# Modulation vectors computed beside later matmul phases instead of in an opening of their own

## The reference, cut to what matters

```python
cond = jax.nn.silu(c)
for l in range(DEPTH):                                   # DEPTH = 2
    ada = (cond @ ada_w[l] + ada_b[l])[:, None, :]       # ada_w[l] is 1024 x 6144, 25 MB
    sh1, sc1, g1, sh2, sc2, g2 = jnp.split(ada, 6, axis=-1)
    h = rms_norm(x, norm1_g[l]) * (1.0 + sc1) + sh1
    x = x + g1 * mixer_sublayer(h, positions, ...)       # 4 token mixers, gates, w_o
    h = rms_norm(x, norm2_g[l]) * (1.0 + sc2) + sh2
    f = swiglu(h, ...) if l % 2 == 0 else moe_swiglu(h, ...)
    x = x + g2 * f
```

## Time and profile before

| | |
|---|---|
| three runs | 6308.77, 6313.16 (median), 6316.53 us |
| profiled execution, span (its own time; the profile gives no other) | 6307.7 us |
| PE busy | 5470.3 us, 87% of the span |
| DVE, ACT, POOL busy | 37%, 30%, 28% |

### The profile page before, as it was taken

The page is one execution under the profiler, slowest core; times in us unless marked ns, Lnnn a source line. Parts: engine busy times, 40 slices in busy tenths (PEclk is TensorE's granted clock), DMA queues, the critical chain, the costliest instruction groups (busy, mean ns, idle before and its releaser), DMA issues. The chain is left out here.

```text
span 6307.7 us, 75191 instructions
## 1 busy us (share of the span) xinstructions
PE 5470.3 (87%) x29832; PEld 4556.7 (72%) x29833; DVE 2332.4 (37%) x1993; ACT 1908.7 (30%) x1541; POOL 1757.5 (28%) x506
## 2 busy tenths in 40 slices
PE   3778779987999977877998499999989999889995
PEld 2527557766778753765776398998989898788984
DVE  8344321113102124432111254433464446654455
ACT  0112111113212111211111144343354345543453
POOL 0130111113344313011111142252354145432442
PEclk6779999998999987999999599999999999999997
DMA  9201011122333320101112256555586557865577
GB/s 388 75 0 27 14 38 46 46 84 78 90 112 96 111 86 0 27 14 37 46 46 85 92 182 205 193 187 187 180 272 207 186 186 261 291 220 192 174 249 251
DMA packets 731573, 829.44 MB, mean 131 GB/s; under 512 B 17362, under 2 KB 646226, under 8 KB 731090
## 3 DMA queue, kind: packets, MB, share of 16 engines
q1 hardware_dynamic: 722306, 792.39, 38.7%
q10 hardware_dynamic: 4560, 18.88, 0.8%
q0 software_dynamic: 4608, 16.78, 0.7%
HBM read 782.89 MB, written 45.09 MB: 131 GB/s over the span
## 5 line engine op out<-in xcount | busy, mean ns | idle before, releaser
L1806 POOL TENSOR_TENSOR e_w_lo<-e_raw,e_w_hi 128x2048 fp32r<-128x2048 f32 x170 | 993.7, 5845 | 1650.3 <-ACT e_w_hi L1742 1650.3
L247 POOL TENSOR_TENSOR w_lo<-w_raw,w_hi 128x1024 fp32r<-128x1024 f32 (+1 forms) x260 | 612.7, 2358 | 2480.2 <-ACT w_hi L242 2480.2
L253 PE MATMUL banks<-h_hi,w_hi 128*128 128x512 f32 x2688 | 1086.9, 404 | 191.1 <-POOL w_lo L247 126.4
L254 PE MATMUL banks<-h_lo,w_hi 128*128 128x512 f32 x2688 | 1057.5, 393 | 0.0
L255 PE MATMUL banks<-h_hi,w_lo 128*128 128x512 f32 x2688 | 1056.5, 393 | 0.0
L253 PE MATMUL banks<-e_x_hi,e_w_hi 128*128 128x256 f32 x3584 | 1020.2, 285 | 35.0 <-issue 26.2
L254 PE MATMUL banks<-e_x_lo,e_w_hi 128*128 128x256 f32 x3584 | 1019.2, 284 | 0.0
L255 PE MATMUL banks<-e_x_hi,e_w_lo 128*128 128x256 f32 x3584 | 1019.1, 284 | 0.0
L1742 ACT ACTIVATE e_w_hi<-e_raw 128x2048 fp32r<-128x2048 f32 x340 | 648.4, 1911 | 511.0 <-PE banks L255 413.5
L253 PEld LDWEIGHTS banks<-h_hi,w_hi 128*128 128x128 f32 x2688 | 511.4, 190 | 326.5 <-issue 154.2
L253 PEld LDWEIGHTS banks<-e_x_hi,e_w_hi 128*128 128x128 f32 x3584 | 693.4, 193 | 38.3 <-issue 28.7
(11 more groups left out here) (276 smaller groups left out, 6303.7 us busy)
## 6 DMA issues: line engine op xcount, KB each, us to landing
e_raw<-in_moe_w_dram SPq DMA_DIRECT2D x508, 1024.0 KB, 5.1
w_raw<-in_ffn_w_dram SPq DMA_DIRECT2D x120, 512.0 KB, 3.8
w_raw<-in_w_in_dram SPq DMA_DIRECT2D x108, 512.0 KB, 4.0
ada_w<-in_ada_w_dram SPq DMA_DIRECT2D x16, 3072.0 KB, 13.2
e_io<-row_scratch SPq DMA_DIRECT2D x13, 1024.0 KB, 6.7
y_scratch<-e_io ACTq DMA_DIRECT2D x12, 1024.0 KB, 4.2
x_res<-x_scratch SPq DMA_DIRECT2D x16, 512.0 KB, 5.5
w_br<-in_w_branch_dram SPq DMA_DIRECT2D x64, 128.0 KB, 3.8
```

The costliest lines, as they stand in the source:

```text
L247: pool.tensor_tensor(m.w_lo[b][:, 0:kt, :], m.w_raw[b][:, 0:kt, :], m.w_hi[b][:, 0:kt, :].bitcast(F32), ALU.subtract).then_inc(s.lo_ready, 1)
L253: pe.matmul(out, wh, rh, start=first, stop=False)
L254: pe.matmul(out, wh, rl, start=False, stop=False)
L1806: eng.tensor_tensor(by_k(w_lo[u]), half_block(q, h), by_k(w_hi[u]).bitcast(F32), ALU.subtract).then_inc(lo_sem[q], 1)
```

## The change

- The opening makes only the first 16 columns of 128 of layer 0's modulation (shift and scale of the first norm): four blocks of 512 columns. `x` is turned half by half straight into `m.x`, where it stays; ACT squares it from PSUM, PE sums the squares, ACT takes the root and DVE the reciprocal there.
- Layer 0's `norm_project_phase` neither loads `x` nor sums squares. SP stores `x` to `xs` after the first two weight blocks, then loads the positions; the rope angles are made by DVE after blocks 1 to 3 and 5 to 7, the sines by ACT after its rounding of blocks 4 and 8. Its loops are written out for both layers.
- The other 32 columns of 128 of layer 0 are made in layer 0's `gate_phase`, one of 128 columns in each of the 32 blocks: SP loads 512 KB, DVE multiplies (128x1024) and reduces over the 8 row tiles. PE sums them over partitions at the start of `out_proj_phase`.
- Layer 1's modulation is made in layer 0's `ffn_phases`: 256 columns (1 MB) in each of the 22 steps of the first half, and two more after the steps of the second half. DVE multiplies and reduces 128x2048; PE sums.

```diff
@@ opening_phase
+            for n, (half, k) in enumerate(steps):
+                if k == 0:
+                    pe.wait_ge(x_in[half], 16)
+                if n >= 4:
+                    pe.wait_ge(s.copied, n - 3)
+                    pe.wait_ge(s.squared, n - 3)
+                for t in range(4):
+                    last = pe.transpose(...)
+                last.then_inc(s.turned, 1)
+                if n:
+                    total(n - 1)             # waits squared; one 512-column product with ones
+            total(len(steps) - 1)
+            for j in range(NB):              # NB = 4
+                pe.wait_ge(s.added, j + 1)
...
+                if j == NB - 2:              # DVE, after block 2
+                    dve.wait_ge(s.root, 1)
+                    dve.reciprocal(rstd[:, :, :], rstd[:, :, :]).then_inc(s.inv, 1)
@@ norm_project_phase, SP of layer 0
+            for j in range(2):
+                w_load(sp, s, m, j, j, w_view(w, cols[j]))
+                for k in range(KT):
+                    sp.dma_start(a.xs[P * k:P * (k + 1), :], m.x[:, k, :]).then_inc(s.stored, 16)
+                sp.wait_ge(s.stored, 16 * KT)
+                sp.wait_ge(s.lo, KT)
+                sp.dma_start(pos_i[:, :], ...).then_inc(s.p_in, 16)
+            for j in range(2, nblocks):
+                w_load(sp, s, m, j, j % 2, w_view(w, cols[j]))
@@ gate_phase, layer 0: SP, then DVE, after each block's own work
+                        sp.wait_ge(s.ada_mult, NBR * mt + n + 1)
+                        sp.dma_start(ada_raw[n % 2][:, :, :], ...)
+                        dve.tensor_tensor(ada_prod[:, :, :], ada_raw[b][:, :, :], cond_wide(m, P), ALU.mult).then_inc(s.ada_mult, 1)
+                        dve.tensor_reduce(m.ada_part[...], ada_prod[:, :, :].rearrange("p k n -> p n k"), AX.X, ALU.add)
@@ out_proj_phase, layer 0: PE, ahead of its blocks
+                for i in range(48 - ADA0):
+                    last = pe.matmul(m.ps[:, 7, i:i + 1], m.ada_part[:, P * i:P * i + P], ones_column)
@@ ffn_phases, layer 0, first part
 SP:
+                def ada_load(j):
+                    sp.wait_ge(s.ada_sum, j + 1)
+                    sp.dma_start(ada_raw[:, :, :], w_view(a.ada_w[l + 1], AW * j, AW)).then_inc(s.ada, 16)
                 with sp.Fori(0, FT) as f:
                     ...                      # the two w_load of step f
+                    if half == 0:
+                        ada_load(f)
 PE:
+                def ada_total(j, at):
+                    pe.wait_ge(s.ada_sum, j + 2)
+                    for i in range(2):
+                        last = pe.matmul(m.ps[:, 7, ds(2 * at + i, 1)], ada_sum[:, P * i:P * i + P], ones_column)
                         ...                  # the 48 matmuls of step f
+                        if half == 0:
+                            ada_total(2 * i + c, 2 * i + c)
 DVE:
+                def ada_part(j):
+                    dve.wait_ge(s.ada, 16 * j + 16)
+                    dve.tensor_tensor(ada_raw[:, :, :], ada_raw[:, :, :], cond_wide(m, AW), ALU.mult).then_inc(s.ada_mult, 1)
+                    dve.wait_ge(s.ada_mult, j + 1)
+                    dve.wait_ge(s.ada_out, j + 1)
+                    dve.tensor_reduce(ada_sum[:, :], ada_raw[:, :, :].rearrange("p k n -> p n k"), AX.X, ALU.add).then_inc(s.ada_sum, 1)
+                dve.sem_inc(s.ada_sum, 1)
                         ...                  # hid, hid_hi, hid_lo of step f
+                        if half == 0:
+                            ada_part(f)
+                if half == 1:
+                    for j in (0, 1):
+                        ada_part(j)          # then bias and scale of layer 1
```

More of the change, by code:

```diff
@@ L113, in constants @@
     return c
+ADA0 = 16
 SEM0 = 104
@@ L282, in opening_phase @@
     cst = m.const
-    GRP = 6
-    W = P * GRP
-    NB = 6 * D // W
+    W = HALF
+    NB = ADA0 * P // W
     xrow = m.place("x_rows", [P, ST, D], F32, m.R)
[L287 to L297, removed]
+    sq = [m.place(f"o_sq{b}", [P, HALF], F32, m.R + (32 + 2 * b) * KB) for b in range(2)]
+    part_sum = [m.place(f"ada_part{b}", [P, W], F32, m.R + (36 + 2 * b) * KB) for b in range(2)]
@@ L299, in _ @@
+    wb = [m.place(f"ada_w{j}", [P, KT, W], F32, m.R + o * KB) for j, o in enumerate((136, 152, 88, 40))]
+    rstd = m.rstd0
+    with phase(nc, "c_in", "id_in", "x_in0", "x_in1", "w0", "w1", "w2", "w3", "turned", "copied", "squared", "totals", "root", "inv",
+               "silu", "scaled", "added", "summed", "folded") as (block, s):
+        w_in = (s.w0, s.w1, s.w2, s.w3)
+        x_in = (s.x_in0, s.x_in1)
+        steps = [(half, k) for half in range(NHALF) for k in range(KT)]
         @block.sync
@@ L303, in _ @@
[L303 to L308, removed]
+            for j in range(NB):
+                sp.dma_start(wb[j][:, :, :], w_view(a.ada_w[0], j * W, W)).then_inc(w_in[j], 16)
@@ L310, in _, with total @@
         @block.tensor
         def _(pe):
[L312 to L319, removed]
+            def total(n):
+                half, k = steps[n]
+                pe.wait_ge(s.squared, n + 1)
+                pe.matmul(m.ps[:, 6 + half, :], cst[:, K_ONE:K_ONE + P], sq[n % 2][:, :],
+                          start=(k == 0), stop=(k == KT - 1)).then_inc(s.totals, 1)
@@ L325, in _ @@
                                      cst[:, K_ONE:K_ONE + 1], start=True, stop=True)
                 last.then_inc(s.summed, 1)
+        @block.scalar
+        def _(act):
+            act.wait_ge(s.c_in, 16)
+            act.activation(m.small[:, S_COND:S_COND + KT], m.small[:, S_COND:S_COND + KT], ACT.Silu).then_inc(s.silu, 1)
+            for n, (half, k) in enumerate(steps):
+                act.wait_ge(s.turned, n + 1)
+                act.activation(m.x[:, k, half * HALF:(half + 1) * HALF], m.ps[:, n % 4, :], ACT.Copy).then_inc(s.copied, 1)
+                if n >= 2:
+                    act.wait_ge(s.totals, n - 1)
+                act.activation(sq[n % 2][:, :], m.ps[:, n % 4, :], ACT.Square).then_inc(s.squared, 1)
+            act.wait_ge(s.totals, len(steps))
+            act.activation(rstd[:, :, :], m.ps[:, 6:8, :], ACT.Sqrt, bias=cst[:, K_EPS:K_EPS + 1], scale=1.0 / D).then_inc(s.root, 1)
@@ L387, in _ @@
[L387 to L407, removed]
@@ L1199, in gate_phase @@
     w = a.w_in[l]
-    with phase(nc, "raw0", "raw1", "br0", "br1", "hi_ready", "lo_ready", "mm_done", "sig_ready", "gated", "summed") as (block, s):
+    ada = l == 0
+    if ada:
+        ada_raw = [m.place(f"g_ada_raw{b}", [P, KT, P], F32, m.R + (136 + 4 * b) * KB) for b in range(2)]
+        ada_prod = m.place("g_ada_prod", [P, KT, P], F32, m.Z0 + 42 * KB)
+    with phase(nc, "raw0", "raw1", "br0", "br1", "hi_ready", "lo_ready", "mm_done", "sig_ready", "gated", "summed",
+               "ada0", "ada1", "ada_mult", "ada_sum") as (block, s):
         @block.sync
@@ L1306, in _ @@
             credit_pe(pe, s)
+            if l == 0:
+                for i in range(48 - ADA0):
+                    last = pe.matmul(m.ps[:, 7, i:i + 1], m.ada_part[:, P * i:P * i + P], m.const[:, K_ONE:K_ONE + 1], start=True, stop=True)
+                last.then_inc(s.ada_sums, 1)
             for j in range(KT):
```

268 lines of the change are left out of this document (173 added, 95 removed).

## The result

Predicted 6481 us (6430 to 6560). The changed kernel takes 6498.18 us (median of four, 6495.6 to 6506.16) against 6313.59 (four, 6308.77 to 6316.53) of the kernel before: 1.0297 times, 95% interval 1.0284 to 1.031. Its profiled span is 6504.4, that of before 6307.7; the profiled execution is the slowest of the four.

What follows compares the result with a forecast made beforehand. PE was taken to bound the FFN steps, DVE the opening's end. Terms -110.3 - 23.4 + 2.6 + 2.4 + 229 + 5.8 + 46 + 16.1 = +168: span 6476, median 6481 us (6430 to 6560).

Steps and rivals of the forecast that it cites:

- The order of the FFN steps: FFN first half: PE waits for DVE's reduction of the same step, a serial chain of 10.9 us, 21 times: +229.
- The sum: Whole kernel: all terms together +168, span 6307.7 to 6476; median 5.5 above the span, so 6481 us.
- rival 3: Opening: PE stays at half clock, so it gains 94 in place of 110.3; whole 6498 us; chance 6%.
- The reduction: FFN steps: DVE's 128x2048 reduction taken as one plain pass, 2.30 us, with no such row to read.
- rival 1: FFN steps: the reduction, reading with a 1 KB step, is slow; at twice the time, 4.6, whole 6537; chance 10%.
- The clock: FFN first half: PE restarts at half clock after each 10 us gap, 2.2 per step, 21 times: +46 (29 to 61).
- The opening: Start of the kernel: with fewer modulation columns made, it ends at 67.4 in place of 177.74 us: -110.3.
- T: Opening: the time at which the 16 steps of transposing and squaring x end, put at 44.5 us.
- its steps go at ACT's 1.3: Opening: variant in which PE's steps keep ACT's pace of 1.3 us in place of 1.5: -113.
- Layer 0's norm: Layer 0 before its first matmul: loading x, squares, root and reciprocal go; 10.5 us left of 33.9: -23.4.
- Gate phase and output projection: Layer 0: only the last gate block's pair is exposed, +2.6; 64 sum records before the output projection, +2.4.
- Second half's tail: FFN second half: the two last pieces stand behind `hid_lo`, the second loading only after the first is reduced: +16.1.

Runs made afterwards that it cites:

- e1: Changed kernel, with DVE making the piece of modulation ahead of its step's hidden block in the FFN steps: 6219.48 us, 0.9853 of the kernel before.
- e5: Changed kernel, FFN reduction summing 8 neighbouring elements in place of 8 lying 1 KB apart (sums wrong, only timing read): 6482.15 us, one run.
- e6: Changed kernel, FFN reduction replaced by three additions of contiguous halves: 6476.92 us, 1.0255 of the kernel before.
- e9: Changed kernel, plus 50 matmuls of 512 columns into an unused bank in each first-half FFN step, before PE's wait: 6466.53 us, 1.0249.
- e2: Changed kernel, plus 40 matmuls of 512 columns into an unused bank in each first-half FFN step, before PE's wait: 6565.17 us, 1.0402.
- e8: As e1, with twelve pieces in each FFN half; in the opening PE sums blocks 0 and 1 between steps, reciprocal after block 3: 6187.71 us, 0.9796.
- e3: Changed kernel, with PE summing each first-half FFN piece two steps later, from two alternating buffers: 6475.33 us, 1.0259 of the kernel before.
- e4: As e3, with SP issuing the piece's load between the step's two weight loads: 6292.98 us, 0.997 of the kernel before.
- e7: As e1, plus 80 one-column matmuls on PE at the start of layer 1's parameter phase: 6247.18 us, 0.989 of the kernel before.
- e10: As e1, plus 40 one-column matmuls on PE at the start of layer 1's parameter phase: 6294.12 us, one run.

## Why the prediction was right, and where its sizes were off

**The order of the FFN steps: right, and shown.** The forecast rested on one reading: one credit, so PE waits for DVE's reduction of the same step, and that stands behind silu and hidden block. The row of PE's 22 waits on `f_ada_sum` shows it; e1 removes it and gives back 279 us of the 299. The 20 that stay are 0.9 a step, about what the prediction put down for PE's own sums (0.60 each in e1, at full clock).

**The sum.** It came to +168 and the profiled span grew by 197, 28 more. The median missed by only 17, and part of that is luck: the prediction puts the median 5.5 above the span, but each execution is 1.8 above its own span, and the profiled one was the slowest, so that the median lies 6 below the profiled span. The median is also the 6498 of rival 3, the opening at half clock, which the ledger refutes; the number alone couldn't have told.

**The reduction: the term that was mis-sized.** Taken at 2.30, it measured 3.59: 1.29 in each step, 28 us, of which 21 count at the end (e5). With the reduction that I had assumed the part takes 530.5, where the prediction had 252.7 + 280.8 = 533.5: the part's miss is this term. e5 shows the step of 1 KB as its cause, e6 that it is on the chain. It is the direction of my rival 1, at 1.6 times the plain pass in place of 2. I had 2.30 although no row reads with a step; nothing spoke for either side, so the value should have stood between.

**The rest of the chain was 0.5 a step shorter** than drawn: the waits average 10.8, of which 3.6 are the reduction, so 7.2 for wake-up, silu, three operations and the multiply, where the prediction had 7.7.

**The clock: right.** A step takes 24.7 on average: 10.9 of matmuls at full clock, 10.8 of wait, 0.9 of sums, and 2.1 left for the half clock; predicted 2.2. e9 gives back 1.9 a step, after 0.7 for its longer filling and with shorter sums. That the clock falls was argued from gaps of 10 us; e2 shows that filling 9 of them doesn't help.

**The opening: right.** T = 41.5 against 44.5 gives 3.0 of the 3.6 that it came out better. That is also what "its steps go at ACT's 1.3" gave (-113), but not for that reason: ACT waited for PE's transposes 14 times, and a step of PE took 1.37 at full clock, not 1.5. With a plain product beside four transposes in each step, PE's records were at full clock from 23 on, so the -94 of an opening at half clock is refuted. The Trainium skill ("TensorE: Matmul & The Clock Gate", on transposes) states that these do not count as busy in the same way; in this mix they did no harm, and no run has a long stretch of transposes alone. e8 confirms the drawn chain: without the wait for PE's sum it ends 9.2 sooner.

**Layer 0's norm: right.** The part up to the gate came out 2.8 worse, but behind the norm. DVE's copy of the tenth projected block starts at 340.59 before and at 203.39 after, 23.3 sooner beyond the opening's gain, as predicted (the first matmul stands 11.1 after the first issue of its weights, not 10.5, and the blocks behind it make up for it). The loss is in two bursts of PE in the mixers; the first two lines are from the kernel before, the others from the changed one:

```profile
745.23 3.71 PE L1016 MATMUL banks<-ws_t,sg_vt 128*64 128x128 f32 x64 [0.91 <-DVE sg_vt L1043]
793.54 3.67 PE L1162 MATMUL banks<-rt_out,const 128*128 128x512 f32 x8 [1.20 <-PEq L130]
```

```profile
608.19 6.06 PE L1066 MATMUL banks<-ws_t,sg_vt 128*64 128x128 f32 x64 [0.78 <-DVE sg_vt L1093]
657.39 5.37 PE L1212 MATMUL banks<-rt_out,const 128*128 128x512 f32 x8 [1.20 <-PEq L132]
```

The same matmuls take 4.0 us more; the granted clock in them was 1.00 before and is 0.52 and 0.68 here. The rest of the layer gives 1.3 back. Why the clock came later I can't say.

**Gate phase and output projection: right** within 1.4. DVE's 3.1 us a block (1.22 and 1.87) is hidden but for the last pair, at 1165.35 and 1166.71; the 64 records of the sums took 13.8 us against 14.5, and didn't warm the clock: the matmuls behind them ran at half clock for another 3.4 us.

**Second half's tail:** 18.1 against 16.1; two reductions at 3.59 are 2.6 more than I had put down.

**Not forecast:** the 9.9 of the rest lie in part 2 of FFN half 1 (+3.0), layer 1 up to its gate (+4.7) and the experts (+3.4), with 1.2 less in part 2 of half 0. Layer 1 up to the gate is 656.0 to 656.8 in e1 to e6 and in e9, so most of that term belongs to the one execution profiled.

## What to carry to other kernels

Before moving work beside a phase that another engine bounds, write down for each engine what stands ahead of it in its order, and count the credits of every wait: here 279 us hung on two lines of DVE's order, and 20 on the added work itself. After one barrier is taken away, look for the next in the DMA queue's own order: a load that waits for a buffer holds up every load behind it (e3 against e4: 185 us). And measure a strided reduction before it goes on a serial chain; contiguous additions did the same for about 1 us less.

## What the runs showed of the hardware that was not expected

- PE's clock fell behind a gap of 1.7 us and a piece's sums, although 9 us of 512-column matmuls at full clock stood right before the gap (e2); with the gap filled it stayed up (e9).
- 64 records of one-column matmuls in 13.8 us, PE busy throughout at clock 0.50, were followed by 3.4 us at half clock.
- A reduction of 128x2048 to 256 outputs takes 3.59 us where its eight elements lie 1 KB apart and 2.29 where they are neighbours (e5); in e1, where it runs beside PE's matmuls and twice the DMA traffic, it took 3.87 (which of these slows it wasn't tried).
- The same expert code cost 2633 to 2637 us or 2695 to 2701, depending on what was added to PE's program ahead of it (e1, e7 and e9 against e2, e3, e4 and e10; e10 is one run).
